# High and low weights of a two-block model, stored element by element in turn

## The chip, the cores and the metric

The kernel runs on one core of one Trainium2 chip. The metric is the device time in microseconds (us) of one execution; for the kernel before it is 2099.25 us, the median of three runs (2098.92 to 2099.32).

## The reference

The program computes two model blocks on 512 tokens of width 1024, all in f32. The first block normalises the input, projects it, and mixes the tokens three ways side by side (a gated recurrence in chunks, attention over neighbours on a grid, attention over 256 memory tokens). It merges the three with gates and adds a feed-forward part of width 2816. The second block has a short convolution mixer, another feed-forward part, an attention with forgetting gates and a last feed-forward part. Cut to the form that matters here:

```python
proj = rms_norm(x, mix_norm_g) @ w_in            # 1024 x 7184
...
x = x + merged @ w_out
x = x + (gelu(dwconv3(a)) * u) @ w_down          # a, u = split(h @ w_up)
...
x = x + (b * causal_dwconv(c * h)) @ a_w_out     # second block
k, v, f = split(rmsnorm(x) @ w_kvf)
x = x + (attention(q, k, v, f) * sigmoid(g)) @ b_w_out
```

Nearly all arithmetic is in the products of activations with weight matrices, and these must keep almost f32 accuracy.

## The kernel before

**Products.** TensorE multiplies in f32 rounded (F32R, printed fp32r), one column per cycle, with fewer bits than f32. To keep accuracy, each operand is split into a high part (rounded to F32R) and a low part (the rest). A product is then three matmuls that add up in the same PSUM bank: high weight x high input, high weight x low input, low weight x high input (L1652, L1653, L1654 in `unit`). Smaller products, such as attention scores and transposes, are plain f32, which TensorE streams at half that pace.

**Units.** A weight matrix is cut into units of 128 partitions x 1024 elements (512 KB): eight blocks of 128 x 128. For each block, TensorE loads a 128 x 128 weight block as its stationary operand (LDWEIGHTS, engine PEld) and streams 512 tokens of input through it (MATMUL, engine PE). A unit is thus 24 matmuls and 24 weight loads. There are 366 units, in the order in which the model needs them; the unit of the three-way merge is half as long in places, and the down projection's units have seven or eight blocks.

**The path of a unit.** Four slots (`NSLOT`) hold units in flight. SP starts the transfer of a unit into `RAW` when GpSimd has finished with the unit four before it (`lo_ready`). ScalarE copies it to the high part `WH`, which rounds it (`hi`, L655), as soon as the transfer has landed and TensorE has finished with the unit four before it (`unit_done`). GpSimd computes the low part `WL` = `RAW` - `WH` in four pieces of 256 elements (`lo`, L519). Then TensorE runs `unit`. All of it is ordered by semaphores and each engine's program is written out in order; no planner moves work.

**The tiles of the change.** `WH` and `WL` are two tiles of 128 partitions x 4 slots x 1024 elements, so that the 128 weights of a block lie in 512 contiguous bytes of a partition. Everything that touches them: `hi` (L655) and its variants for the output projection of the second block (L932, L940) write `WH`; `lo` (L519) and its variants (L529 for the forget gates, L540 for the gates of the recurrence, L628) read `WH` and write `WL` or a spare part of `WH`; the matmuls of L1652 to L1654, L1770 and L1771, L1828 to L1853, L1889 to L1891, L1949 and L1950, and L2049 to L2051 load them as the stationary operand.

One stage uses them the other way round. `value_blocks` (L1965 to L1967) makes the attention's values with tokens as rows. There, input blocks `XH` and `XL` are stationary, and 512 columns of `WH` or `WL` are the moving operand; these eight units are numbered from `U["fv"]`.

Of the kernel before, what the change touches and what calls it, by code (L numbers as in the profile page):

```python
# [12 lines left out]
F32 = mybir.dt.float32  # L13
F32R = mybir.dt.float32r
ALU = mybir.AluOpType
ACT = mybir.ActivationFunctionType
AX = mybir.AxisListType

P = 128
D = 1024  # L20
KB = D // P
# [6 lines left out]
NSLOT = 4  # L28
LO_PARTS = 4
UW = KB * P  # L30
# [119 lines left out]
U, O = {}, {}  # L150
# [38 lines left out]
def two_blocks(nc, A, out):  # L189
# [4 lines left out]
    def fixed(name, shape, dt=F32):  # L194
        t = nc.alloc_sbuf_tensor_at(name, shape, dt, offset=top[0])
        n = 4
        for d in shape[1:]:
            n *= d
        top[0] += (n + 31) // 32 * 32
        return t  # L200
# [13 lines left out]
    XH = fixed("XH", [P, KB, S], F32R)  # L214
    XL = fixed("XL", [P, KB, S], F32R)
    RAW = fixed("RAW", [P, NSLOT, UW])
    WH = fixed("WH", [P, NSLOT, UW], F32R)
    WL = fixed("WL", [P, NSLOT, UW], F32R)
    R = fixed("R", [P, S])
    RM = fixed("RM", [P, M])  # L220
    SS = fixed("SS", [P, S])
# [81 lines left out]
    bank = [nc.alloc_psum_tensor(f"bank{b}", [P, S], F32) for b in range(8)]  # L303
# [11 lines left out]
    hi_ready, lo_ready, unit_done = sem("hi_ready"), sem("lo_ready"), sem("unit_done")  # L315
# [67 lines left out]
    def width(u):  # L383

        j = u - U["merge"]
        return UW // 2 if 0 <= j < len(MRG) and MRG[j][0] == "br" else UW

    def blk(t, n):

        return t[:, bass.ds(n, 1), :].rearrange("p o s -> p (o s)")  # L390
# [121 lines left out]
    def _(pool):  # L512
        def lo(u0, j, i, per):
            s = (u0 + j) % NSLOT
            pool.wait_ge(hi_ready, i * per + (u0 + j + 1))
            parts = LO_PARTS * width(u0 + j) // UW
            for c in range(parts):
                w = slice(c * UW // LO_PARTS, (c + 1) * UW // LO_PARTS)
                last = nc.gpsimd.tensor_tensor(WL[:, s, w], RAW[:, s, w], WH[:, s, w].bitcast(F32), ALU.subtract)  # L519
                if u0 == 0 and j < 2 and c < parts - 1:  # L520
                    last.then_inc(first_lo[j], 1)
            last.then_inc(lo_ready, 1)

        def lo_forget():

            s = U["f"] % NSLOT
            pool.wait_ge(hi_ready, U["f"] + 1)
            raw, w = (t[:, s, :].rearrange("p (k c) -> p k c", c=P) for t in (RAW, WH))
            nc.gpsimd.tensor_tensor(w[:, :, 32:48], raw[:, :, 0:16], w[:, :, 0:16].bitcast(F32), ALU.subtract)\  # L529
                .then_inc(lo_ready, 1)  # L530

        def lo_gate(u):

            s = u % NSLOT
            pool.wait_ge(hi_ready, u + 1)
            raw, w = (t[:, s, :].rearrange("p (n c) -> p n c", c=32) for t in (RAW, WH))
            pool.wait_ge(r_ready, 1)
# [27 lines left out]
        for u in range(NATT):  # L565
# [4 lines left out]
            if u in BIAS_UNITS:  # L570

                p, v = BIAS_UNITS[u]
# [50 lines left out]
        def lo_parted(n):  # L623
# [3 lines left out]
            for w in [slice(c * 2 * P, min((c + 1) * 2 * P, KEND)) for c in range(LO_PARTS)]:  # L627
                nc.gpsimd.tensor_tensor(WL[:, s, w], RAW[:, s, w], WH[:, s, w].bitcast(F32), ALU.subtract)  # L628
            nc.gpsimd.tensor_tensor(WEL[:, n, :], RAW[:, s, KEND:UW], WEH[:, n, :].bitcast(F32), ALU.subtract)\
# [14 lines left out]
    def _(act):  # L644
        A_ = nc.scalar.activation

        def hi(u0, j, i, per):

            if not isinstance(i, int) or u0 + j + i * per < NUNITS:
                s = (u0 + j) % NSLOT  # L650
                act.wait_ge(raw_full[s], i * (16 * per // NSLOT) + 16 * ((u0 + j) // NSLOT + 1))
                if u0 + j >= NSLOT:
                    act.wait_ge(unit_done, i * per + (u0 + j - NSLOT + 1))
                w = slice(0, width(u0 + j))
                A_(WH[:, s, w], RAW[:, s, w], ACT.Copy).then_inc(hi_ready, 1)  # L655

        AHEAD = 3
        LN_EXP = "natural_log_exp_and_others"
# [51 lines left out]
        for t, (un, st) in enumerate(SLOTS):  # L710
            u = UIDX[un] if un else None
# [20 lines left out]
            if m < 4 * ML_H:  # L732

                h, s = m // 4, m % 4
# [8 lines left out]
                for d in range(2):  # L743
                    w = slice(P * s, S) if d == 0 else slice(0, P * (s + 1))
                    A_(SXM[m % 2][:, d, w], UE[:, h, d, w], ACT.Relu, bias=UT[:, s, 32 * d + h:32 * d + h + 1])
                act.drain()
                for d in range(2):
                    w = slice(P * s, S) if d == 0 else slice(0, P * (s + 1))
                    e = SXM[m % 2][:, d, w]
                    last = A_(e, e, ACT.Exp, scale=-1.0)  # L750
# [24 lines left out]
            if 1 in finishing(st):  # L775
                h = st[1] - 1
# [9 lines left out]
                for q in range(TB):  # L786
                    last = A_(HQ[:, q, :], HQ[:, q, :], ACT.Copy, scale=HS[:, q:q + 1])
                last.then_inc(h_rs, 1)
            if un and un[0] in HALF:
                k = sum(1 for x in UNITS[:u] if x[0] in HALF)  # L790
# [10 lines left out]
            if t and EXTRA[t - 1][:1] and EXTRA[t - 1][0][:2] == ("tr", "nav"):  # L801

                p = EXTRA[t - 1][0][2]
# [121 lines left out]
        def hi_parted(n):  # L925
# [4 lines left out]
            if n == 0:  # L930
                act.wait_ge(fc_out, 16)
            A_(WH[:, s, 0:KEND], RAW[:, s, 0:KEND], ACT.Copy)  # L932
            A_(WEH[:, n, :], RAW[:, s, KEND:UW], ACT.Copy).then_inc(hi_ready, 1)
# [700 lines left out]
    def _(pe):  # L1634
        mm = nc.tensor.matmul

        def unit(u0, j, i, per, kc, xh, xl, k0, dst, start=True, stop=True, width=S, ready=None, halfway=None):
# [4 lines left out]
            for k in range(kc):  # L1642
# [10 lines left out]
                mm(dst[:, 0:width], WH[:, s, w], b, start=False, stop=False)  # L1653
                last = mm(dst[:, 0:width], WL[:, s, w], a, start=False, stop=stop and k == kc - 1)  # L1654
            last.then_inc(unit_done, 1)
# [118 lines left out]
        for t, (un, st) in enumerate(SLOTS):  # L1774
            before = SLOTS[t - 1][1] if t else None
            if st and st[0] in ("xa", "na"):
                kind, p, s = st
# [3 lines left out]
                for j in range(2):  # L1781
                    if g >= 1:
                        pe.wait_ge(s_read, 2 * g + j - 1)
                    if kind == "xa":
                        h = 2 * p + j
                        mm(SB[j][:, 0:M], XQ[:, h, P * s:P * (s + 1)], MK[:, h, :], start=True, stop=True)\
                            .then_inc(s_full, 1)
                    else:
                        r = slice(64 * j, 64 * j + 64)
                        mm(SB[j][:, 0:M], QN[r, p % 2, P * s:P * (s + 1)], KN[r, p % 2, KEY0[s]:KEY0[s] + M],  # L1790
                           start=True, stop=True)\
                            .then_inc(s_full, 1)
            if st and st[0] == "ml":
                _, h, s = st
# [17 lines left out]
            if un:  # L1812
# [5 lines left out]
                if t == 0:  # L1818
                    for n, (tt, part, ks) in enumerate(START_ORDER):
# [3 lines left out]
                        for k in ks:  # L1823
                            w = slice(k * P, (k + 1) * P)
                            ends = n == START_LAST[tt] and k == KB - 1
                            if part == "h":
                                pe.wait_ge(xh_ready, k + 1)
                                last = mm(bb[:], WH[:, tt, w], XH[:, k, :], start=k == 0, stop=False)  # L1828
                            elif part == "l":
                                pe.wait_ge(split_ready, k + 1)  # L1830
                                last = mm(bb[:], WH[:, tt, w], XL[:, k, :], start=False, stop=ends)
                            else:
                                if tt < 2 and k < KB - 2:
                                    pe.wait_ge(first_lo[tt], k // 2 + 1)
                                else:
                                    pe.wait_ge(lo_ready, tt + 1)
                                last = mm(bb[:], WL[:, tt, w], XH[:, k, :], start=False, stop=ends)
                        if n == START_LAST[tt]:
# [5 lines left out]
                elif t < 5:  # L1844
                    b = mixer_bank(o)
                    pe.wait_ge(hi_ready, t + 1)
                    for k in range(KB):
                        w = slice(k * P, (k + 1) * P)
# [3 lines left out]
                    for k in range(KB):  # L1852
                        last = mm(b[:], WL[:, t % NSLOT, k * P:(k + 1) * P], XH[:, k, :], start=False, stop=k == KB - 1)  # L1853
# [99 lines left out]
        def value_blocks(h, u, blocks):  # L1953

            n = 4 * h + u
            slot = (U["fv"] + n) % NSLOT
            pe.wait_ge(lo_ready, U["fv"] + n + 1)
            for t in blocks:
                if h and u == 0:
                    pe.wait_ge(f_v, t + 1)  # L1960
                for kk in range(2):
                    k = 2 * u + kk
                    a, b = XH[:, k, t * P:(t + 1) * P], XL[:, k, t * P:(t + 1) * P]
                    w = slice(kk * S, (kk + 1) * S)
                    mm(bank[2 + t][:], a, WH[:, slot, w], start=k == 0, stop=False)  # L1965
                    mm(bank[2 + t][:], b, WH[:, slot, w], start=False, stop=False)  # L1966
                    last = mm(bank[2 + t][:], a, WL[:, slot, w], start=False, stop=k == KB - 1)  # L1967
                if t == TB - 1:
                    last.then_inc(unit_done, 1)
                elif u == 3:  # L1970
                    last.then_inc(v_full, 1)
# [96 lines left out]
        for t in range(TB):  # L2068
            last = mm(bank[6][:, 2 * t:2 * t + 2], SS[:, t * P:(t + 1) * P], ONES[:, 0:2], start=True, stop=True)
# [149 lines left out]
```

## Time and profile before

| what | value |
|---|---|
| median of three runs | 2099.25 us |
| span of the profiled execution, first to last instruction | 2098.1 us |
| TensorE matmul busy (PE) | 2090.3 us, 100% |
| TensorE weight load busy (PEld) | 1709.4 us, 81% |
| VectorE, ScalarE, GpSimd busy | 46%, 42%, 56% |
| matmuls, weight loads | 9860, 9860 |

The profile was taken in one execution. Its own time is the span, 2098.1 us, and what lies around it; the median of the runs is 1.15 us above the span. Records of matmuls overlap, because the next one begins to stream before the results of the one before are out, so the price of a matmul in a dense stretch is the distance from start to start, and not the length of its record. A weight load's record lies beside the matmul before it.

### The profile page before, as it was taken

How to read it: one execution, taken by the hardware profiler on the slowest of the kernel's cores; microseconds unless marked ns; L12 is line 12 of the kernel's file. 1: busy time of each engine (PE TensorE's matmuls, PEld its weight loads, DVE VectorE, ACT ScalarE, POOL GpSimd, SP SyncE). 2: the span in 40 equal slices, each digit the busy share in tenths (PEclk: the TensorE clock that was granted, in tenths of full speed). 3: DMA queues.
4: the chain of work that ended last, by engine and by line, in shares of the span. 5: the costliest groups of instructions: out<-in, count | busy, mean ns of one | idle time of the engine just before them, and what ended most of it. 6: DMA issues, size and time to landing. Idle time of an engine off the chain costs nothing.

```text
span 2098.1 us, 29633 instructions
## 1 busy us (share of the span) xinstructions
PE 2090.3 (100%) x9860; PEld 1709.4 (81%) x9860; DVE 972.7 (46%) x1682; ACT 884.3 (42%) x1355; POOL 1164.5 (56%) x1554
## 2 busy tenths in 40 slices
PE   9999999999999999999999999999999999999999
PEld 7788888888888888888888888888777778888887
DVE  6567564334455551234445544213377755545300
ACT  5544556223434343332244344224466655434321
POOL 8553346556555556555455656565544536556653
PEclk9999999999999999999999999999999999999999
DMA  6333222323332333323233333333322213333332
GB/s 234 119 99 114 63 64 70 106 78 123 92 100 93 96 94 102 95 91 100 91 101 100 96 94 89 108 94 101 111 81 81 81 61 101 100 100 90 103 92 76
DMA packets 62667, 203.70 MB, mean 97 GB/s; under 512 B 7056, under 2 KB 8720, under 8 KB 62576
## 3 DMA queue, kind: packets, MB, share of 16 engines
q1 hardware_dynamic: 60624, 201.54, 30.9%
q10 hardware_dynamic: 1952, 0.99, 0.2%
q8 instruction: 52, 0.85, 0.2%
q14 instruction: 39, 0.32, 0.0%
HBM read 199.42 MB, written 2.26 MB: 96 GB/s over the span
## 4 chain that ended last, share of the span: by engine, by line
PE 98%; DVE 1%; DMA 0%; DVEq 0%; ACT 0%; issue 0%; ACTq 0%; SPq 0%
PE bank L1652 28%; PE bank L1654 28%; PE bank L1653 28%; PE bank L1992 1%; PE bank L2018 1%; PE bank L1761 1%; PE bank L2004 1%; PE bank L1706 1%; PE bank L1965 1%; PE bank L1967 1%; PE bank L1966 1%; PE bank L1891 1%; PE bank L1889 1%; PE bank L1890 1%; PE bank L2049 1%; PE bank L1802 1%
## 5 line engine op out<-in xcount | busy, mean ns | idle before, releaser
L519 POOL TENSOR_TENSOR WL<-RAW,WH 128x256 fp32r<-128x256 f32 x1424 | 1105.8, 809 | 865.7 <-ACT WH L655 858.8
L1652 PE MATMUL bank<-XH,WH 128*128 128x512 f32 x1688 | 661.2, 392 | 0.3 <-DVE FG L1571 0.3
L1654 PE MATMUL bank<-XH,WL 128*128 128x512 f32 x1688 | 657.2, 389 | 0.0
L1653 PE MATMUL bank<-XL,WH 128*128 128x512 f32 x1688 | 656.9, 389 | 0.0
L655 ACT ACTIVATE WH<-RAW 128x1024 fp32r<-128x1024 f32 (+1 forms) x366 | 372.9, 1023 | 236.1 <-PE bank L1654 208.4
L1652 PEld LDWEIGHTS bank<-XH,WH 128*128 128x128 f32 x1688 | 316.9, 188 | 68.4 <-issue 2.8
L1654 PEld LDWEIGHTS bank<-XH,WL 128*128 128x128 f32 x1688 | 316.9, 188 | 66.7
L1653 PEld LDWEIGHTS bank<-XL,WH 128*128 128x128 f32 x1688 | 317.0, 188 | 64.5
L1652 PE MATMUL bank<-FH,WH 128*128 128x512 f32 x528 | 205.4, 389 | 0.0
L1653 PE MATMUL bank<-FL,WH 128*128 128x512 f32 x528 | 205.4, 389 | 0.0
L1654 PE MATMUL bank<-FH,WL 128*128 128x512 f32 x528 | 205.4, 389 | 0.0
L1399 DVE TENSOR_TENSOR X<-X,bank 128x512 f32 (+1 forms) x48 | 32.9, 685 | 292.4 <-PE bank L1654 283.9
L882 ACT ACTIVATE TD<-TC 128x512 f32<-128x512 f32 x66 | 41.7, 632 | 278.0 <-DVE TC L1143 188.0
L1143 DVE SCALAR_TENSOR_TENSOR TC<-TA,PAR,TC 128x511 f32<-128x511 f32 (+1 forms) x134 | 108.9, 813 | 22.4 <-issue 21.8
L1653 PEld LDWEIGHTS bank<-FL,WH 128*128 128x128 f32 x528 | 99.1, 188 | 20.7
L1654 PEld LDWEIGHTS bank<-FH,WL 128*128 128x128 f32 x528 | 99.1, 188 | 20.7
L1652 PEld LDWEIGHTS bank<-FH,WH 128*128 128x128 f32 x528 | 99.1, 188 | 20.4
L1429 DVE TENSOR_TENSOR TA<-bank,R 128x512 f32<-128x512 f32 x66 | 45.6, 691 | 124.1 <-PE bank L1654 116.1
L1434 DVE TENSOR_TENSOR TE<-bank,R 128x512 f32<-128x512 f32 x66 | 45.6, 691 | 110.0 <-PE bank L1654 110.0
L885 ACT ACTIVATE FH<-TA 128x512 f32 x66 | 41.8, 633 | 126.3 <-DVE TA L1438 126.3
L1440 DVE TENSOR_TENSOR FL<-TA,FH 128x512 f32 x66 | 60.1, 911 | 61.7 <-ACT FH L885 61.7
L849 ACT ACTIVATE XH<-X,PAR (+1 forms) x40 | 29.0, 724 | 134.9 <-DVE X L1399 134.9
(336 smaller groups left out, 2618.5 us busy)
## 6 DMA issues: line engine op xcount, KB each, us to landing
RAW<-in_w_up SPq DMA_DIRECT2D x132, 512.0 KB, 3.5
RAW<-in_w_att SPq DMA_DIRECT2D x50, 512.0 KB, 3.6
RAW<-in_w_down SPq DMA_DIRECT2D x48, 448.0 KB, 3.2
RAW<-in_w_down SPq DMA_DIRECT2D x24, 512.0 KB, 3.5
RAW<-in_w_ain SPq DMA_DIRECT2D x24, 512.0 KB, 3.4
RAW<-in_w_fa SPq DMA_DIRECT2D x24, 512.0 KB, 3.6
RAW<-in_w_mrg SPq DMA_DIRECT2D x15, 512.0 KB, 3.9
RAW<-in_w_mrg SPq DMA_DIRECT2D x24, 256.0 KB, 2.7
```

What stands on the lines that cost most here:

```text
L519: last = nc.gpsimd.tensor_tensor(WL[:, s, w], RAW[:, s, w], WH[:, s, w].bitcast(F32), ALU.subtract)
L655: A_(WH[:, s, w], RAW[:, s, w], ACT.Copy).then_inc(hi_ready, 1)
L882: A_(TD[:], TC[:], fn).then_inc(glu_ready, 1)
L885: A_(blk(FH, i * 2 + n), TA[:], ACT.Copy).then_inc(ffh_ready, 1)
L1143: last = v.scalar_tensor_tensor(out=TC[:, -d:S], in0=c[:, 0:S + d], scalar=w[k], in1=TC[:, -d:S], op0=ALU.mult, op1=ALU.add)
L1399: v.tensor_tensor(blk(X, nn), blk(X, nn), b[:], ALU.add).then_inc(lin_free, 1)
L1429: v.tensor_tensor(TA[:], LB[0 if (O[name] % 2) == 0 else 1][:], R[:], ALU.mult)\
L1434: v.tensor_tensor(TE[:], LB[1 if (O[name] % 2) == 0 else 0][:], R[:], ALU.mult)\
L1440: v.tensor_tensor(blk(FL, nn), TA[:], blk(FH, nn).bitcast(F32), ALU.subtract).then_inc(ffl_ready, 1)
L1652: mm(dst[:, 0:width], WH[:, s, w], a, start=start and k == 0, stop=False)
L1653: mm(dst[:, 0:width], WH[:, s, w], b, start=False, stop=False)
L1654: last = mm(dst[:, 0:width], WL[:, s, w], a, start=False, stop=stop and k == kc - 1)
```

## The change

High and low weights share one tile, `WHL`, of 2 x 1024 elements a slot. Element 2n is the high part of weight n, element 2n + 1 its low part; `WH` and `WL` become views with a step of two elements, 8 bytes. Every access through these names now steps 8 bytes: ScalarE's writes, GpSimd's reads and writes, and TensorE's weight loads. For the eight units of the value blocks the same memory is used in two contiguous halves, `WPH` and `WPL`; a helper, `weights`, picks the views by the unit's number. The tiles take as much memory as before. No instruction, wait or transfer is added, removed or moved.

```diff
-    WH = fixed("WH", [P, NSLOT, UW], F32R)
-    WL = fixed("WL", [P, NSLOT, UW], F32R)
+    WHL = fixed("WHL", [P, NSLOT, 2 * UW], F32R)
+    WPAIR = WHL[:].rearrange("p s (n h) -> p s n h", h=2)
+    WH, WL = WPAIR[:, :, :, 0], WPAIR[:, :, :, 1]
+    WPH, WPL = WHL[:, :, 0:UW], WHL[:, :, UW:2 * UW]
...
+    def weights(u):
+
+        return (WPH, WPL) if U["fv"] <= u < U["fa"] else (WH, WL)
...
-                last = nc.gpsimd.tensor_tensor(WL[:, s, w], RAW[:, s, w], WH[:, s, w].bitcast(F32), ALU.subtract)
+                h, l = weights(u0)
+                last = nc.gpsimd.tensor_tensor(l[:, s, w], RAW[:, s, w], h[:, s, w].bitcast(F32), ALU.subtract)
...
-                A_(WH[:, s, w], RAW[:, s, w], ACT.Copy).then_inc(hi_ready, 1)
+                A_(weights(u0 + j + (i * per if isinstance(i, int) else 0))[0][:, s, w], RAW[:, s, w], ACT.Copy).then_inc(hi_ready, 1)
...
-                    mm(bank[2 + t][:], a, WH[:, slot, w], start=k == 0, stop=False)
-                    mm(bank[2 + t][:], b, WH[:, slot, w], start=False, stop=False)
-                    last = mm(bank[2 + t][:], a, WL[:, slot, w], start=False, stop=k == KB - 1)
+                    mm(bank[2 + t][:], a, WPH[:, slot, w], start=k == 0, stop=False)
+                    mm(bank[2 + t][:], b, WPH[:, slot, w], start=False, stop=False)
+                    last = mm(bank[2 + t][:], a, WPL[:, slot, w], start=False, stop=k == KB - 1)
```

## Rows read from the trace of the kernel before

**Rows 1.** The page: span, engine totals (busy us, share, instructions), chain by engine.

```profile
span 2098.1 us, 29633 instructions
PE 2090.3 (100%) x9860; PEld 1709.4 (81%) x9860; DVE 972.7 (46%) x1682; ACT 884.3 (42%) x1355; POOL 1164.5 (56%) x1554
...
PE 98%; DVE 1%; DMA 0%; DVEq 0%; ACT 0%; issue 0%; ACTq 0%; SPq 0%
```

**Rows 2.** The page's costliest groups: xcount, busy us, mean ns, idle before, releaser.

```profile
L519 POOL TENSOR_TENSOR WL<-RAW,WH 128x256 fp32r<-128x256 f32 x1424 | 1105.8, 809 | 865.7 <-ACT WH L655 858.8
L1652 PE MATMUL bank<-XH,WH 128*128 128x512 f32 x1688 | 661.2, 392 | 0.3 <-DVE FG L1571 0.3
...
L655 ACT ACTIVATE WH<-RAW 128x1024 fp32r<-128x1024 f32 (+1 forms) x366 | 372.9, 1023 | 236.1 <-PE bank L1654 208.4
L1652 PEld LDWEIGHTS bank<-XH,WH 128*128 128x128 f32 x1688 | 316.9, 188 | 68.4 <-issue 2.8
```

**Rows 3.** Timeline of PE, from 1000 us: start us, length us.

```profile
1000.06 0.39 PE L1652 MATMUL bank<-XH,WH 128*128 128x512 f32 x1
...
1003.46 0.39 PE L1652 MATMUL bank<-XH,WH 128*128 128x512 f32 x1
```

**Rows 4.** Span and mean granted TensorE clock.

```profile
core 0: 2098.1 us, clock 1.000
```

**Rows 5.** Timeline of PEld in the same stretch.

```profile
1000.06 0.19 PEld L1653 LDWEIGHTS bank<-XL,WH 128*128 128x128 f32 x1
```

**Rows 6.** Timeline of PE, plain f32 matmuls, two in each row.

```profile
907.85 1.02 PE L1666 MATMUL bank<-TC,ONER 128*128 128x512 f32 x2
908.71 1.02 PE L1668 MATMUL bank<-SS,ONER 128*128 128x512 f32 x2
```

**Rows 7.** Timeline of PE, 256 columns: a matmul and the eighth after it.

```profile
84.08 0.28 PE L1652 MATMUL bank<-MH,WH 128*128 128x256 f32 x1
...
85.04 0.28 PE L1654 MATMUL bank<-MH,WL 128*128 128x256 f32 x1
```

**Rows 8.** A pause: L1891 from 505 us (min/median/max ns), timelines of PE and PEld.

```profile
L1891 PE MATMUL bank<-GH,WL x5: 388/389/389, 504.7 to 507.4; 128*128 128x512 f32 x5
...
507.38 0.39 PE L1891 MATMUL bank<-GH,WL 128*128 128x512 f32 x1
507.99 0.50 PE L1652 MATMUL bank<-GH,WH 128*128 128x512 f32 x1 [0.22 <-DVE X L1399]
...
507.99 0.19 PEld L1652 LDWEIGHTS bank<-GH,WH 128*128 128x128 f32 x1 [0.64 <-DVE X L1399]
508.10 0.19 PEld L1653 LDWEIGHTS bank<-GL,WH 128*128 128x128 f32 x1
```

**Rows 9.** The first matmul of L1828 alone, and timelines of PE and PEld there.

```profile
L1828 PE MATMUL bank<-XH,WH x1: 473/473/473, 7.3 to 7.3; 128*128 128x512 f32 x1
...
7.34 1.02 PE L1828 MATMUL bank<-XH,WH 128*128 128x512 f32 x2 [0.89 <-ACT XH L685]
...
7.31 0.19 PEld L1828 LDWEIGHTS bank<-XH,WH 128*128 128x128 f32 x1 [1.05 <-issue]
7.86 0.19 PEld L1828 LDWEIGHTS bank<-XH,WH 128*128 128x128 f32 x1 [0.36 <-ACT XH L685]
```

**Rows 10.** View by tile, matmuls that read WH: duration ns min/median/max, first and last start.

```profile
L1653 PE MATMUL bank<-XL,WH x1688: 387/389/402, 38.7 to 1974.5; 128*128 128x512 f32 x188
...
L1653 PE MATMUL bank<-AHL,WH x176: 387/389/402, 1044.3 to 1667.4; 128*128 128x512 f32 x176
...
L1965 PE MATMUL bank<-WH,XH x64: 389/389/486, 1436.3 to 1484.3; 128*128 128x512 f32 x64
```

**Rows 11.** Weight loads of 48 columns.

```profile
L1949 PEld LDWEIGHTS bank<-XH,WH 128*48 128x48 f32 x8 | 1.0, 122 | 0.8
```

**Rows 12.** GpSimd subtractions of 512 elements: contiguous, and in runs of 16.

```profile
L589 POOL TENSOR_TENSOR YL<-Y,YH 128x512 fp32r<-128x512 f32 x8 | 10.1, 1285 | 15.2 <-ACT YH L770 15.2
L540 POOL TENSOR_TENSOR WH<-RAW,WH 128x512 fp32r<-128x512 f32 x1 | 1.3, 1283 | 0.1
```

## The prediction

> **What bounds the kernel now.** I read the engine totals and the chain of waits first. TensorE is busy for 2090.3 of 2098.1 us, and 98% of the chain that ended last is TensorE itself: at almost no point does it wait for weights, for a transfer or for another engine [rows 1]. So only two things can move the time: the distance from one matmul to the next, or an engine beside TensorE becoming slower than TensorE.
>
> Next the costliest groups. The three matmuls of a weight block (high weight with high input, high with low, low with high) make up nearly everything; each has a weight load of its own, 188 ns long, beside a matmul whose record is 389 ns long [rows 2]. Records overlap, so the real price of a matmul is the distance of starts: from 1000.06 to 1003.46 us lie 15 matmuls, 3.40 us / 15 = 226.7 ns each [rows 3]. The granted clock is 1.000 over the span, the 2.4 GHz level [rows 4], so 512 columns at one per cycle would be 512 / 2.4 = 213.3 ns. Each matmul thus has 13.3 ns, 32 cycles, that are not columns. These 13.3 ns are the only thing on the path that a different weight layout can touch.
>
> Whose are they? The load of the next block starts with the matmul before it: L1653's load at 1000.06 us, with L1652's matmul [rows 3, 5]. So it runs inside that stream. Three places tell something.
> - Matmuls of plain f32, which take two cycles a column, have almost none of it: from 907.85 to 908.71 us two of them, 430 ns each, against 1024 / 2.4 = 426.7 [rows 6]. They too have a load beside them. So a load beside a stream is not dear by itself.
> - With 256 columns in fp32r the distance is (85.04 - 84.08) / 8 = 120 ns against 106.7 for the columns [rows 7]. Again 13.3 ns: the surplus goes with the matmul, not with its length. And a load every 120 ns is sustained, so a load occupies its path for 120 ns at most.
> - The last matmul before a pause, at 507.38 us, has no load beside it, since the next block is taken up at 507.99. If the load beside it were what lengthens a stream, its record should be some 13 ns shorter. It has the shortest of its window, 388 ns against 389 [rows 8]. Likewise the matmul at 7.34 us: its own load starts at 7.31, the next load at 7.86, after the 473 ns of its record; from its load's start to its end that is 0.50 us [rows 9]. The matmul at 507.99 starts with its load, has the next load inside it from 508.10 on, and ends after the same 0.50 us [rows 8].
>
> So the surplus looks like a fixed price at the start of an fp32r matmul, and not like something that the load of the next block takes from it. That speaks for no change. It is not proof: records of the same matmul spread from 387 to 402 ns [rows 10], so something in the meeting of loads and streams does vary, and ends are modelled.
>
> **The change part by part.**
> *Weight loads.* Each L1652 to L1654 has 1688 + 528 + 176 + 96 + 64 + 48 = 2600 loads, one for each matmul in the view by tile [rows 10] (two of its six groups are shown), three lines 7800; L2049 to L2051, L1889 to L1891 and the first units add 524. So 8324 of 9860 loads now step 8 bytes. The 192 matmuls of the value blocks keep contiguous weights as moving operand (64 at each of three lines) [rows 10]; the norm sums, transposes and attention products load other tiles. No load or matmul is added. Each nanosecond on the distance is worth 8.3 us, 0.4%.
> The trace has no load with a step, so I bound it. What a load costs per column: 48 columns take 122 ns, 128 take 188 [rows 2, 11], so (188 - 122) / 80 = 0.83 ns a column. Lower end: 0, the step costs nothing. Upper end: every column twice, 106 ns more, a record of 294 ns. The path of the load would then be taken for 120 + 106 = 226 ns out of 226.7: just hidden. If its fixed part doubled too, 240 ns, 13.3 ns a matmul would come out on the path, 111 us. I take 0, since the room for even a doubling is there.
>
> *ScalarE.* It writes the high weights at a step of 8 bytes. A copy takes 1023 ns, the mean over full and half units [rows 2]. A unit of 24 matmuls lasts 24 x 226.7 = 5.44 us on TensorE. Doubled, 2.1 us: still hidden, since ScalarE is at 42% [rows 1] and works up to three units ahead in four slots. I take 0.
>
> *GpSimd.* It reads the high weights and writes the low ones at 8 bytes, four pieces a unit, 809 ns each [rows 2], 3.24 us of 5.44. It becomes the bound from 5.44 / 4 = 1360 ns a piece, in the 21-matmul units of the down projection from 21 x 226.7 / 4 = 1190 ns. The nearest row with a broken pattern is the gate unit, 512 elements in runs of 16 with gaps: 1283 ns, against 1285 for 512 contiguous [rows 12]. So a gap costs nothing there; the lower end is 0, the upper end a doubling, 1618 ns. I take 0, by that row.
> The Trainium skill, GPSIMD Engine Reference, section 7 (Performance pitfalls for Q7 kernels), charges about half more for reads whose step is over 8 bytes and nothing up to 8, which this change just meets. If the chip charged it here all the same, a piece would be 809 x 1.5 = 1214 ns, hidden everywhere but in the down units, where 4 x 1214 - 4760 = 96 ns on 72 units would show as 7 us at most; by the rule itself the term is 0. No run here shows such a read.
>
> *Slots, transfers, waits.* Four slots as before; transfers land in the raw tile, which is untouched. No wait is added or moved, so nothing new stands behind one.
>
> Sum: 0 on loads + 0 on ScalarE + 0 on GpSimd. The profiled execution's span is 2098.1 us; the median of the runs is 2099.25, 1.15 above it. Forecast 2099.2 us, with a range of its own of 2096 to 2103.
>
> **The rivals.**
> *Loads and streams get in each other's way less (faster).* The 32 cycles are a quarter of 128 columns, and 128 weights of 4 bytes are 32 pieces of 16 bytes: the price could be one cycle for each place where the load and the moving read meet, and a load that walks through memory at twice the pace could meet it in another rhythm. For it: plain f32, which reads its moving operand at half the pace, has hardly any surplus [rows 6], and the records spread [rows 10]. Against it: the matmuls without a load beside them are no shorter [rows 8, 9]. Price: all of it 13.3 x 8324 = 111 us, 1988; down to the surplus of plain f32 (3 ns) 86 us, 2013; I put this case at half, 6.7 ns, 55 us: 2044.
>
> *The same meeting costs more (slower).* If the price goes by the stretch of memory that a load covers, 1024 bytes in place of 512 make 64 cycles of surplus: a distance of 240 ns, 13.3 x 8324 = 111 us, 2210; if half of the new pieces are dodged, 2155. It decides from the first nanosecond, on every unit's matmuls alike. For and against it the same rows speak as before, and the path of the load that could just take a doubling ends at the same 240 ns.
> The Trainium skill, SBUF — State Buffer, section Specifications (TRN2), has lines of 16 bytes, wants two hits in each for full bandwidth, and says that each crossing to a new line pays a penalty. A step of 8 bytes keeps two hits, by which the forecast holds; it also crosses twice as often, by which this rival does. No run here shows lines.
>
> *GpSimd becomes the bound (slower).* At 1618 ns a piece a unit takes 6.47 us, 1.03 more than its matmuls, on some 350 units 360 us: 2460. It decides from 1360 ns, a factor of 1.68. Against it the gate unit's row [rows 12].
>
> **How the numbers follow.** No change: 0.42. Less in each other's way: 0.30. More: 0.23. GpSimd: 0.05. Within 0.2% (4 us, about what a measurement of this kernel can tell from none) is the forecast's own case, 0.42; faster 0.30; slower 0.23 + 0.05 = 0.28. For a range that holds 8 in 10, I take the halves of both middle rivals and some way past them, 2030 to 2185; outside are a full gain (about 0.06), a full doubling (about 0.09) and GpSimd.
>
> **What would show it.** The distance of matmul starts in the same stretch: 226.7 ns if the forecast is right, 213 to 222 for the first rival, 232 to 240 for the second. The load's record: 188 ns if the step is free, up to 294 if columns are read twice. GpSimd's piece: near 809 ns, and TensorE waiting for GpSimd in the chain only if it passes 1360. The value blocks, whose loads stay contiguous, must keep 226.7 in every case; if they move as well, the reason is not the load's step.

## The result, and the profile after

| kernel | median us | span of the profiled execution, us |
|---|---|---|
| before | 2099.28 (2098.92 to 2099.50, 4 runs) | 2098.1 |
| after | 2150.65 (2150.14 to 2151.05, 4 runs) | 2149.1 |

The ratio is 1.0244, with an interval of 1.0230 to 1.0259: slower by 51 us, where no change was forecast. One execution of e8 below (3389.49 us, at a mean granted clock of 0.577) fell in a slow state and stands in no comparison. The line numbers of the kernel after are those of before plus 7 (L1652 is L1659, L519 is L526), and high and low weights carry one name, `WHL`.

The page of after: engine totals and chain, then the costliest groups (count, busy us, mean ns of one, idle before). They answer to [rows 1, 2].

```profile
PE 2142.2 (100%) x9860; PEld 1754.9 (82%) x9860; DVE 975.8 (45%) x1682; ACT 912.7 (42%) x1355; POOL 1172.2 (55%) x1554
...
PE 99%; DVE 1%; DMA 0%; ACT 0%; DVEq 0%; issue 0%; SPq 0%; ACTq 0%
...
L526 POOL TENSOR_TENSOR WHL<-RAW,WHL 128x256 fp32r<-128x256 f32 x1424 | 1113.6, 814 | 907.6 <-ACT WHL L662 901.9
L1659 PE MATMUL bank<-XH,WHL 128*128 128x512 f32 x1688 | 669.3, 397 | 0.3 <-DVE FG L1578 0.3
...
L662 ACT ACTIVATE WHL<-RAW 128x1024 fp32r<-128x1024 f32 (+1 forms) x366 | 401.2, 1100 | 241.5 <-PE bank L1661 213.3
L1659 PEld LDWEIGHTS bank<-XH,WHL 128*128 128x128 f32 x1688 | 326.1, 193 | 70.2 <-issue 2.8
```

TensorE still is the whole chain, and no other engine has come near it: GpSimd's piece went from 809 to 814 ns, ScalarE's copy from 1023 to 1100, the weight load's record from 188 to 193. So the distance of matmuls must have grown. The timeline of PE in after, where [rows 3] stand for before:

```profile
1000.17 0.39 PE L1659 MATMUL bank<-XH,WHL 128*128 128x512 f32 x1
...
1003.67 0.39 PE L1659 MATMUL bank<-XH,WHL 128*128 128x512 f32 x1
```

15 matmuls take 3.50 us: 233.3 ns each, against 226.7. The granted clock is 1.000 as before (2.4 GHz), so 544 cycles have become 560. Which matmuls moved is read from the view by tile (record ns min/median/max, first and last start), whose rows answer to [rows 10]:

```profile
L1660 PE MATMUL bank<-XL,WHL x1688: 392/394/399, 39.4 to 2022.1; 128*128 128x512 f32 x188
...
L1660 PE MATMUL bank<-ML,WHL x64: 278/283/288, 84.9 to 143.5; 128*128 128x256 f32 x64
...
L1972 PE MATMUL bank<-WHL,XH x64: 389/389/486, 1472.9 to 1520.9; 128*128 128x512 f32 x64
```

Records of 512 columns went from 389 to 394 ns. The value blocks (L1972), whose stationary operand is still contiguous, kept 389 ns. Their distance in the timeline of PE in after is (1493.65 - 1490.25) / 15 = 226.7 ns, as before:

```profile
1490.25 0.39 PE L1972 MATMUL bank<-WHL,XH 128*128 128x512 f32 x1
...
1493.65 0.39 PE L1972 MATMUL bank<-WHL,XH 128*128 128x512 f32 x1
```

The 256-column matmuls have stepped loads too, yet kept the distance of 120 ns of [rows 7]: in the timeline of PE in after, (85.49 - 84.89) / 5 = 120 ns.

```profile
84.89 0.28 PE L1660 MATMUL bank<-ML,WHL 128*128 128x256 f32 x1
...
85.49 0.28 PE L1659 MATMUL bank<-MH,WHL 128*128 128x256 f32 x1
```

The sum closes. Some 8045 dense distances of 512-column matmuls that load stepped weights, times 6.67 ns, are 53.7 us. Against that the matmuls just after a pause lose less than before: counted over the trace, these distances in sum lay 2.5 us above 226.7 ns each in before and 0.2 us below 233.3 ns each in after. 53.7 - 2.7 = 51.0 us; the spans differ by 51.0.

### The profile page after: what moved, and what is told of

Same layout as the page of the kernel before. It is cut to its first block, busy times and chain, and to the rows that moved or that the text cites. A ratio compares the mean times of both kernels' runs of the same rounds, so it can differ in the third digit from the quotient of the medians.

```text
span 2149.1 us, 29633 instructions
## 1 busy us (share of the span) xinstructions
PE 2142.2 (100%) x9860; PEld 1754.9 (82%) x9860; DVE 975.8 (45%) x1682; ACT 912.7 (42%) x1355; POOL 1172.2 (55%) x1554
## 4 chain that ended last, share of the span: by engine, by line
PE 99%; DVE 1%; DMA 0%; ACT 0%; DVEq 0%; issue 0%; SPq 0%; ACTq 0%
PE bank L1659 28%; PE bank L1661 28%; PE bank L1660 28%; PE bank L1999 1%; PE bank L2025 1%; PE bank L1768 1%; PE bank L2011 1%; PE bank L1713 1%; PE bank L2056 1%; PE bank L1972 1%; PE bank L1974 1%; PE bank L1898 1%; PE bank L1973 1%; PE bank L1896 1%; PE bank L1897 1%; PE bank L2058 1%
## 5 line engine op out<-in xcount | busy, mean ns | idle before, releaser
L526 POOL TENSOR_TENSOR WHL<-RAW,WHL 128x256 fp32r<-128x256 f32 x1424 | 1113.6, 814 | 907.6 <-ACT WHL L662 901.9
L1659 PE MATMUL bank<-XH,WHL 128*128 128x512 f32 x1688 | 669.3, 397 | 0.3 <-DVE FG L1578 0.3
L1661 PE MATMUL bank<-XH,WHL 128*128 128x512 f32 x1688 | 665.2, 394 | 0.0
L1660 PE MATMUL bank<-XL,WHL 128*128 128x512 f32 x1688 | 665.2, 394 | 0.0
L662 ACT ACTIVATE WHL<-RAW 128x1024 fp32r<-128x1024 f32 (+1 forms) x366 | 401.2, 1100 | 241.5 <-PE bank L1661 213.3
L1659 PEld LDWEIGHTS bank<-XH,WHL 128*128 128x128 f32 x1688 | 326.1, 193 | 70.2 <-issue 2.8
L1661 PEld LDWEIGHTS bank<-XH,WHL 128*128 128x128 f32 x1688 | 326.0, 193 | 67.8
L1660 PEld LDWEIGHTS bank<-XL,WHL 128*128 128x128 f32 x1688 | 326.1, 193 | 66.1
L1661 PE MATMUL bank<-FH,WHL 128*128 128x512 f32 x528 | 208.0, 394 | 0.0
L1659 PE MATMUL bank<-FH,WHL 128*128 128x512 f32 x528 | 208.0, 394 | 0.0
L1660 PE MATMUL bank<-FL,WHL 128*128 128x512 f32 x528 | 208.0, 394 | 0.0
L1659 PEld LDWEIGHTS bank<-FH,WHL 128*128 128x128 f32 x528 | 101.9, 193 | 21.4
L1660 PEld LDWEIGHTS bank<-FL,WHL 128*128 128x128 f32 x528 | 101.9, 193 | 21.3
L1661 PEld LDWEIGHTS bank<-FH,WHL 128*128 128x128 f32 x528 | 101.9, 193 | 21.2
```

The source lines that it names most:

```text
L526: last = nc.gpsimd.tensor_tensor(l[:, s, w], RAW[:, s, w], h[:, s, w].bitcast(F32), ALU.subtract)
L662: A_(weights(u0 + j + (i * per if isinstance(i, int) else 0))[0][:, s, w], RAW[:, s, w], ACT.Copy).then_inc(hi_ready, 1)
L1659: mm(dst[:, 0:width], WH[:, s, w], a, start=start and k == 0, stop=False)
```

## The experiments

All times are set against the kernel before on the same chip. In e1 and e2, theory A lays the price on the loads and theory B on the copies. From e3 on, the expectations weigh two kinds of theory about the loads: a toll (the theories A), which each load pays for its own step, and a pattern (theory B), by which the load's addresses and the moving operand's reads fall into a rhythm with more or fewer waits.

### e1: loads contiguous again, copies stepped

```diff
-                mm(dst[:, 0:width], WH[:, s, w], a, start=start and k == 0, stop=False)
-                mm(dst[:, 0:width], WH[:, s, w], b, start=False, stop=False)
-                last = mm(dst[:, 0:width], WL[:, s, w], a, start=False, stop=stop and k == kc - 1)
+                mm(dst[:, 0:width], WPH[:, s, w], a, start=start and k == 0, stop=False)
+                mm(dst[:, 0:width], WPH[:, s, w], b, start=False, stop=False)
+                last = mm(dst[:, 0:width], WPL[:, s, w], a, start=False, stop=stop and k == kc - 1)
```

(and so at L1896 to L1898 and L2056 to L2058)

> The changed kernel, but 8172 of its 8324 stepped weight loads read 512 contiguous bytes of the slot; both copies still write at 8 bytes (so the weights that are multiplied are not the matrix's). Theory A, the load's step lengthens the stream by 6.7 ns: the distance goes back to 226.7 ns and the time to 2099 + 152 x 6.7 ns = 2100 us. Theory B, the stepped copies of ScalarE and GpSimd disturb TensorE's reads: distance 233.3 ns, time 2150 us as in the changed kernel.

Measured: 2099.89 us, ratio 1.0002 (0.9993 to 1.0012). The page of e1, GpSimd and ScalarE, and a row of its view by tile:

```profile
L526 POOL TENSOR_TENSOR WHL<-RAW,WHL 128x256 fp32r<-128x256 f32 x1424 | 1120.8, 819 | 851.5 <-ACT WHL L662 846.2
L662 ACT ACTIVATE WHL<-RAW 128x1024 fp32r<-128x1024 f32 (+1 forms) x366 | 399.7, 1096 | 229.7 <-PE bank L1661 202.6
...
L1659 PE MATMUL bank<-FH,WHL x528: 388/389/390, 781.0 to 2094.2; 128*128 128x512 f32 x176
```

Both engines pay for their steps as in after (819 and 1096 ns), while the matmuls' records and the time are those of before. So the copies cost the kernel nothing that shows, and the price is with the loads.

### e2: copies contiguous, loads stepped

```diff
-        return (WPH, WPL) if U["fv"] <= u < U["fa"] else (WH, WL)
+        return (WH, WL) if u < 5 else (WPH, WPL)
```

(and both copies ask for the views of each unit's own number)

> The counterpart: the loads step 8 bytes as in the changed kernel, the copies of all units from the sixth on write contiguous halves (the weights that are multiplied are again not the matrix's). Theory A, the load's step: distance 233.3 ns, time about 2150 us. Theory B, the copies: 226.7 ns, about 2100 us.

Measured: 2149.95 us, ratio 1.0241 (1.0224 to 1.0259), with ScalarE's copy back at 1023 ns. The view by tile:

```profile
L1659 PE MATMUL bank<-FH,WHL x528: 394/394/394, 797.2 to 2144.0; 128*128 128x512 f32 x176
```

The mirror image of e1: with the copies contiguous but for the first units, the stepped loads alone make the whole price (50.5 us over the kernel before on the same chip).

### e3: a sweep of TensorE alone

35 stretches of 48 dense matmuls each, all else left out. `w(offset, (step, count))` is the load, `m(...)` the moving operand, in elements of 4 bytes; both tiles lie on the same grid.

```python
for i in R: last = mm(bank[0][:], w(128 * (i % 8), (1, P)), m(512 * (i % 8), (1, S)), start=i == 0, stop=i == N - 1)
for i in R: last = mm(bank[1][:], w(256 * (i % 8), (2, P)), m(512 * (i % 8), (1, S)), start=i == 0, stop=i == N - 1)
```

> Only streams on TensorE, 35 stretches of 48 matmuls one behind the other, each with its own load; no other engine works beside them and the model is not computed. Theory A1, a toll by the stretch of memory that the load covers, 16 cycles for each 512 bytes on top of 16 fixed: step 1, 2, 3, 4, 5, 6, 8 give 226.7, 233.3, 240, 246.7, 253, 260, 273 ns, step 0 gives 220, 64 columns at step 1 give 223; the direction of the moving operand changes nothing. Theory A2, a toll by 16-byte lines touched, at most one per column: as A1 up to step 4, then constant at 246.7. [...] In the stretch where only every fourth load steps 16 bytes, the distance that is longer is that of the matmul during which this load runs if the load takes from the stream beside it, and that of its own matmul if the stream waits for it.

The timeline of PE in e3. A row joins 32 matmuls: start, and time from the first start to the last end; less one record, over the steps between the starts, it is the distance (L53: (7.63 - 0.39) / 31 = 233.5 ns). The table's values come from the unrounded starts.

```profile
34.66 7.63 PE L53 MATMUL bank<-X,W 128*128 128x512 f32 x32
...
45.89 7.70 PE L54 MATMUL bank<-X,W 128*128 128x512 f32 x32
...
80.19 7.58 PE L57 MATMUL bank<-X,W 128*128 128x512 f32 x32
...
169.64 7.63 PE L65 MATMUL bank<-X,W 128*128 128x512 f32 x32
...
240.12 14.69 PE L71 MATMUL bank<-X,W 128*128 128x512 f32 x32
...
346.71 7.07 PE L79 MATMUL bank<-X,W 128*128 128x512 f32 x32
...
357.32 7.63 PE L80 MATMUL bank<-X,W 128*128 128x512 f32 x32
...
374.27 7.63 PE L82 MATMUL bank<-X,W 128*128 128x256 f32 x32
...
448.95 7.42 PE L86 MATMUL bank<-X,W 128*128 128x512 f32 x32
```

Mean distance of the 17th to 48th start in each stretch:

| load | moving operand | line | distance, ns |
|---|---|---|---|
| contiguous | ascending | L86 | 226.7 |
| step 8 bytes | ascending | L53 | 233.3 |
| step 12, 16, 32 bytes | ascending | L54 to L56 | 235.6, 235.1, 245.4 |
| one address | ascending | L57 | 231.7 |
| contiguous, 64 or 32 columns | ascending | L62, L64 | 230.2, 231.7 |
| contiguous, 8 bytes later | ascending | L60 | 230.7 |
| contiguous, 8 bytes, 16 bytes, one address | descending | L65 to L68 | 233.3 each |
| contiguous | one address | L79 | 215.8 |
| step 16 bytes | one address | L80 | 233.3 |
| step 16 bytes | ascending, 256 columns | L82 | 233.3 |
| contiguous | step 8 bytes | L71 | 453.2 |

The sweep repeats the kernel's two numbers with TensorE alone (226.7 and 233.3), so nothing else in the kernel is needed. The tolls fall: a load from one address, or of a quarter of the columns, should be the cheapest, and is dearer than the contiguous one; with a descending stream the load's step is indifferent; a contiguous load that merely begins 8 bytes later is dearer. With one load in four at a step of 16 bytes (L84) no fourth distance stands out, neither of the two that the expectation names: all lie between 231 and 235 ns, 233.4 in the mean. And where the moving operand is one address, 215.8 ns remain, 518 cycles for 512 columns: all but 6 cycles of the surplus go with the walk of the moving operand. The step of 16 bytes has a limit of its own besides: such loads follow each other every 233.3 ns, whether 256 columns or a single moving address stand against them (L82, L80).

### e4: a third of the loads contiguous

```diff
-                last = mm(dst[:, 0:width], WL[:, s, w], a, start=False, stop=stop and k == kc - 1)
+                last = mm(dst[:, 0:width], WPL[:, s, w], a, start=False, stop=stop and k == kc - 1)
```

(and so at L1898 and L2058)

> The changed kernel, but the loads of the low weights, one in three, read 512 contiguous bytes (not the matrix's weights). Theory A, each stepped load lengthens the stream beside it by 6.7 ns, independently of its neighbours: the distance after the second matmul of a block, during which the contiguous load runs, is 226.7 ns, the other two 233.3; about 2150.6 - 2724 x 6.7 ns = 2132.5 us. Theory A', the price falls on the load's own matmul: the same time, but the distance after the third is the short one. Theory B, the distances are a rhythm that a load's pattern pulls the stream into: no distance need be 226.7 or 233.3, and the time need not lie at a third of the way.

Measured: 2148.52 us, ratio 1.0232 (1.0215 to 1.0249). A price per stepped load would have given back a third of it, 2132.5. The timeline of PE in e4:

```profile
849.95 0.39 PE L1659 MATMUL bank<-FH,WHL 128*128 128x512 f32 x1
...
852.75 0.39 PE L1659 MATMUL bank<-FH,WHL 128*128 128x512 f32 x1
```

2.80 us for four blocks, 12 matmuls: 233.3 ns each. The stream as a whole keeps its distance when one load in three is contiguous. So the price is not a sum over the stepped loads, as a toll would have it.

### e5: more of the sweep

39 stretches: columns, moving orders, offsets, types. The lines for 384 columns with a stepped load and for weights that begin 64 bytes late:

```python
for i in R: last = mm(bank[1][:, 0:384], w(256 * (i % 8), (2, P)), m(512 * (i % 8), (1, 384)), start=i == 0, stop=i == N - 1)
...
for i in R: last = mm(bank[4][:], w(16 + 128 * (i % 8), (1, P)), m(512 * (i % 8), (1, 512)), start=i == 0, stop=i == N - 1)
```

> Only streams on TensorE again, 39 stretches of 48 matmuls. (1) Moving operand from a single address, loads at step 2: if the surplus is waiting in the moving operand's reads, 216 ns as for step 1; if the load alone makes it, 222 to 223. (2) 448, 384, 320, 256 columns: if the surplus is a fixed price per matmul, as the prediction has it, 200, 173.3, 146.7, 120 ns at step 1; if it goes with the columns (17 cycles for 16), 198.3, 170, 141.7, 113.3 ns unless the load is the limit. At step 2: 13.3 ns less per 32 columns either way, from 233.3. (3) bf16 and plain f32, whose moving operand needs half the bytes in a given time: no more than 3 ns between contiguous loads and loads at 8 bytes, if the surplus is a matter of how fast the moving operand is read. (4) Other offsets and other orders of the moving operand's columns: a theory of a fixed price has 226.7 and 233.3 everywhere; a theory of meetings has other values, and some may lie below 226.7.

The timeline of PE in e5: 512 columns with a contiguous and a stepped load (L55, L56), one moving address with a stepped load (L58), 384 columns with either (L60, L64), bf16 with either (L89, L90), plain f32 with a stepped one (L92).

```profile
27.00 7.42 PE L55 MATMUL bank<-X,W 128*128 128x512 f32 x32
37.99 7.63 PE L56 MATMUL bank<-X,W 128*128 128x512 f32 x32
...
59.28 7.07 PE L58 MATMUL bank<-X,W 128*128 128x512 f32 x32
...
78.76 5.88 PE L60 MATMUL bank<-X,W 128*128 128x384 f32 x33
...
109.64 5.88 PE L64 MATMUL bank<-X,W 128*128 128x384 f32 x33
...
381.94 7.07 PE L89 MATMUL bank<-XB,WB 128*128 128x512 bf16 x32
392.30 7.07 PE L90 MATMUL bank<-XB,WB 128*128 128x512 bf16 x32
...
446.85 13.90 PE L92 MATMUL bank<-X,W 128*128 128x512 f32 x32
```

The step of 8 bytes is free in bf16 (215.8 ns both ways), in plain f32 (429.2 both ways), with one moving address (215.8 both ways) and at 384, 320 and 256 columns (173.3, 146.7, 120.0 both ways). At 448 columns the stepped load is even the cheaper one, 203.3 against 206.7 ns. So of these streams only those in fp32r whose moving operand walks have something to lose, and how much depends on the length of the stream as well. With contiguous loads, operands moved against each other by 256, 512 or 1024 bytes kept 226.7; weights moved by 64 bytes went to 233.4 without any step (L75). Eleven other orders of the moving operand's columns (L78 to L88) had 226.7 to 277.7 ns; none was shorter than the plain ascending one. Where contiguous and stepped loads alternate, the mean is 230.2 ns (L67), which a sum of tolls would give too (230.0); with one stepped load in four it is 231.7 (L68), where the sum gives 228.3.

### e6: the layout of before, 32 bytes off the grid

```diff
+    top[0] = (top[0] + line - 1) // line * line - 32
+    WH = fixed("WH", [P, NSLOT, UW], F32R)
+    WL = fixed("WL", [P, NSLOT, UW], F32R)
+    RC = fixed("RC", [P, 2 * TB])
     top[0] = (top[0] + line - 1) // line * line
     X = fixed("X", [P, KB, S])
```

(their old places are removed)

> The kernel before with contiguous weights, both weight tiles moved as a whole to lie 32 bytes lower against the 512-byte grid on which the input tiles lie; nothing else changes and the model is computed in full. Theory A, the step of the load costs the 6.7 ns: no step, so 226.7 ns and 2099 us. Theory B, the distance depends on how the load's addresses meet the moving operand's: the sweep's nearest stretch (moving operand 32 bytes higher, step 1) had 233.3 ns, so about 2099 + 8324 x 6.6 ns = 2154 us, as slow as the changed kernel without any step.

Measured: 2150.40 us, ratio 1.0242 (1.0225 to 1.0259). The timeline of PE in e6:

```profile
1000.02 0.39 PE L1653 MATMUL bank<-XH,WH 128*128 128x512 f32 x1
...
1003.52 0.40 PE L1653 MATMUL bank<-XH,WH 128*128 128x512 f32 x1
```

3.50 us over 15 matmuls: 233.3 ns, without one of the change's stepped accesses. The price of the change can thus be had without the change: what counts is where the load's addresses lie against the moving operand's.

### e7: where the weights begin

36 stretches over the load's first address (48 elements are 192 bytes) and over lengths of 464, 480 and 496 columns:

```python
for i in R: last = mm(bank[4][:], w(48 + 128 * (i % 8), (1, P)), m(512 * (i % 8), (1, 512)), start=i == 0, stop=i == N - 1)
...
for i in R: last = mm(bank[5][:], w(16 + 256 * (i % 8), (2, P)), m(512 * (i % 8), (1, 512)), start=i == 0, stop=i == N - 1)
```

> Only streams on TensorE, 36 stretches of 48 matmuls, loads at step 1 and step 2 with 25 starting offsets, and 496, 480 and 464 columns. Theory A, a price of the step: every step 1 has 226.7 ns, every step 2 has 233.3. Theory B, a meeting by address: step 1 has 226.7 only for offsets that are a multiple of 256 bytes and 228 to 234 at others; if it can be won as well as lost, some offset lies below 226.7 (220 would be 16 cycles of surplus in place of 32), and that offset would be worth 6.7 ns x 8324 = 55 us in the model's kernel.

Measured, contiguous load beginning so many bytes past the 256-byte grid: 0: 226.7; 4: 232.5; 8: 230.8; 16 to 112: 231.9 to 234.4; 128 and 160: 233.5; 192: 228.9; 224: 233.3; 240: 226.7; 256 and 768: 226.7 ns. With the step of 8 bytes: 0, 16, 96, 256, 512: 233.3; 8: 231.7; 32: 231.9; 64: 230.0; 128: 231.4; 192: 233.5. With 496, 480 and 464 columns: 220.0, 216.7 and 208.8 ns contiguous, 225.3, 220.0 and 211.6 with the step. At 512 columns none of the starts and steps tried gave less than 226.7, so the sweep offered no better layout to run. The timeline of PE in e7: 192 bytes past the grid (L64), 240 past it (L66), stepped 64 past it (L73), stepped 256 past it (L77).

```profile
157.04 7.48 PE L64 MATMUL bank<-X,W 128*128 128x512 f32 x32
...
179.18 7.42 PE L66 MATMUL bank<-X,W 128*128 128x512 f32 x32
...
256.55 7.52 PE L73 MATMUL bank<-X,W 128*128 128x512 f32 x32
...
301.15 7.63 PE L77 MATMUL bank<-X,W 128*128 128x512 f32 x32
```

### e8 and e9: two starts from the sweep, in the whole kernel

e8 is e6 with 64 in place of 32 (192 bytes past a 256-byte mark; one more small tile fills the gap); e9 is the kernel after with its tile moved likewise:

```diff
+    top[0] = (top[0] + line - 1) // line * line - 192
+    WHL = fixed("WHL", [P, NSLOT, 2 * UW], F32R)
```

(its views follow it, and its old place is removed)

> The kernel before with contiguous weights, its high and low weights put 64 bytes below the 512-byte grid on which the inputs lie (the whole model is computed). Theory B (the address pattern of the load against the moving operand's reads sets how often the stream waits, and the pattern counts as in the third sweep): 64 bytes below the grid is 192 bytes past the last 256-byte mark, where the sweep had 228.9 ns; the shift by 32 bytes turned 6.6 ns on the distance into 51 us, so 2.2 ns give 17 us, 2116 us. Rival (on the grid 226.7 ns, off it 233.3, nothing between in a whole kernel whose three matmuls read different inputs): 2150 us. Rival (only distances below 64 bytes count): 2099 us.

> The changed kernel with the shared tile put 192 bytes below the 512-byte grid, that is 64 bytes past a 256-byte mark; weight loads still step 8 bytes (the whole model is computed). Theory B: the third sweep had 230.0 ns for a step of 8 bytes at this start, 3.3 ns above 226.7 and half of what the step costs on the grid, so about 2099 + 25 = 2125 us: faster than the changed kernel by an address alone. The value blocks, whose moving operand is shifted too, go from 226.7 to about 228.9 ns (first sweep, moving operand 64 bytes past). Rival (the step costs by itself, wherever the tile lies): 2150.7 us and value blocks at 226.7.

Measured: e8 ran 2116.35, 2119.40 and 2124.06 us, ratio 1.0087 (1.0065 to 1.0108); e9 2127.88 (2127.53 to 2129.49), ratio 1.0134 (1.0116 to 1.0152). The medians, 2119.40 and 2127.88, lie 3 us above what the sweep gave and far from 2150; and e9 makes the changed kernel 23 us faster by an address alone. That the tiles stand in another order in e6 is not its price: e8 has the same order. The value blocks fit too: in e6 and e8, where their moving operand is the shifted tile, their distance went from 226.7 to 233.3 ns. What the sweep had not shown stands in the timeline of PE in e8, the same line and tiles in the first feed-forward part and in the second:

```profile
699.61 0.40 PE L1653 MATMUL bank<-XH,WH 128*128 128x512 f32 x1
...
703.11 0.40 PE L1653 MATMUL bank<-XH,WH 128*128 128x512 f32 x1
...
1200.20 0.39 PE L1653 MATMUL bank<-XH,WH 128*128 128x512 f32 x1
...
1203.64 0.39 PE L1653 MATMUL bank<-XH,WH 128*128 128x512 f32 x1
```

3.50 / 15 = 233.3 ns in the one, 3.44 / 15 = 229.3 in the other. From 549 to 920 us the stream keeps 233.3 from one pause to the next; elsewhere mostly 228.9. e9 does the same with 233.3 (352 to 514 and 922 to 1059 us) and 230.0, and the changed kernel has short stretches of 235.5 (343 to 353 us). One layout can settle in two rhythms, and in these profiles it changed only across a pause. The profiled execution of e8, 2124.06 us, is 8 us above the sweep's figure, and the long stretch makes 7 of them (1592 distances, 4.4 ns each); that of e9, 2129.49 us, is 4 above, and its two stretches make 4 (1283 distances, 3.3 ns each). The differences between e8's runs may be of the same kind; the others have no profile. The value blocks of e9, whose moving operand is shifted against its stationary one, went to about 229 ns as expected; the timeline of PE in e9:

```profile
1470.11 0.39 PE L1973 MATMUL bank<-WHL,XH 128*128 128x512 f32 x1
...
1473.54 0.39 PE L1973 MATMUL bank<-WHL,XH 128*128 128x512 f32 x1
```

(3.43 / 15 = 228.7.)

## Why the prediction was wrong

**The step that failed.** "So the surplus looks like a fixed price at the start of an fp32r matmul, and not like something that the load of the next block takes from it." From this the loads were priced at 0, "since the room for even a doubling is there": the load was bounded by how long it keeps its own path busy, and not by what its addresses do to the stream beside it. The term measured 51 us, 6.67 ns on each distance of 512 columns (e1, e2). Of the 32 cycles of surplus in before, 6 are there when the moving operand stands still (215.8 ns); the other 26 go with its walk, and 16 more come with the load's addresses (e3, e6).

**Why the evidence misled.**
- Plain f32 [rows 6] was read as: a load beside a stream is harmless. It is harmless there even with a step (429.2 ns, e5), as it is in bf16. By the distances, both read about 2 bytes of moving operand a cycle and fp32r nearly 4 (each plain f32 product leaves two records of 429 ns, 96 for 48 products in e5, so it takes four cycles a column in all); that this is why they are spared fits, but was not tested. The row said nothing on fp32r.
- The 256 columns [rows 7] were read as: the surplus is the same at every length. With contiguous loads the sweeps have 32 surplus cycles at 256, 320, 384, 496 and 512 columns, but 48 at 448 (496 cycles), 40 at 480 and 37 at 464. Two lengths that agreed hid that.
- The matmuls without a load beside them [rows 8, 9] kept their record of 388 ns, where the stream with one moving address has 379 (L79, L58). So these rows may even be right that the 26 cycles need no load; no experiment ran a stream without loads. They could not tell what another load pattern would add.

**What spoke against it and was passed over.** The prediction saw the records spread from 387 to 402 ns [rows 10] and went on. Where they spread was to be seen in the kernel before, right behind the pause of [rows 8], in the timeline of PE:

```profile
508.33 0.40 PE L1653 MATMUL bank<-GL,WH 128*128 128x512 f32 x1
...
510.88 0.39 PE L1652 MATMUL bank<-GH,WH 128*128 128x512 f32 x1
...
512.92 0.39 PE L1652 MATMUL bank<-GH,WH 128*128 128x512 f32 x1
```

From 508.33 to 510.88 lie 11 distances of 231.8 ns, from there to 512.92 nine of 226.7: same tiles, same clock, same loads. 226.7 is what the stream settles to, not what a matmul costs. The matmuls of the very loads of [rows 11], 48 contiguous columns, say it more plainly, in the timeline of PE in before:

```profile
1440.38 0.40 PE L1949 MATMUL bank<-XH,WH 128*48 128x512 f32 x1
...
1441.32 0.40 PE L1949 MATMUL bank<-XH,WH 128*48 128x512 f32 x1
```

Four distances take 0.94 us, 235 ns each: these loads are 66 ns shorter than those of 128 columns, and the stream beside them is 8 ns a matmul slower. A fixed price would have left it at 226.7. With the step, in after, the same 16 matmuls have 230.3 ns.

**The load's room.** The room was there, and not needed: stepped loads at 256 columns follow each other every 120 ns as the contiguous ones do (e5), and the record grew by 5 ns, not 106. The near doubling that was priced comes at a step of 16 bytes (records of 310 ns, 330 at 32 bytes in e3; one load every 233.3 ns in place of 120), and even so 512 columns hide most of it (235.1 ns).

**The sums.** The 8324 loads that a nanosecond was multiplied by include 192 of 256-column matmuls, which lost nothing, and those at pauses; some 8045 remain. The 7 us set as a ceiling for GpSimd in the down projection count all 72 units, of which 48 have seven blocks, so it would be 5 us. Neither moves the forecast.

**The rivals.** "The same meeting costs more (slower)" had the sign and, at half price, the size: 2155 against 2150.65, and through it the range of 2030 to 2185 holds the result. That was luck: its mechanism, a price by the stretch of memory that a load covers, is not what was found. e6 covers the old 512 bytes and pays the same, and a load from a single address pays too (231.7). The first rival's "another rhythm" was the nearer picture, with the other sign. The Trainium skill, SBUF — State Buffer, section Specifications (TRN2), wants two hits in each 16-byte line. The load's own pace obeys it: 120 ns at 256 columns with the step of 8 bytes, 233.3 with 16. The stream does not: the same 8-byte step as moving operand doubles the distance (453.2 ns, L71), and it is e6, with none but contiguous loads of these weights, that loses as much as the change. The measurement decides: the rule prices neither.

**What held.** ScalarE's and GpSimd's terms are 0 on the path (e1), with 1100 ns against 1023 and 814 against 809. The Trainium skill, GPSIMD Engine Reference, section 7 (Performance pitfalls for Q7 kernels), charges for a read's step only above 8 bytes; the 814 ns agree. The value blocks kept 226.7. TensorE stayed the only bound.

**What stays open.** Shown is that the load's addresses against the moving operand's set the distance. By what mechanism they do it, why 544 and 560 cycles are so often the settled values, and whether a load is needed for the first 26 cycles, was not shown.

## What to carry to other kernels

In a dense fp32r stream the settled distance of starts depends on how weight loads lie against the moving operand: keep contiguous stationary and moving tiles on one grid of 256 bytes (226.7 ns here at each of its starts that was tried), and after a change of layout read the distance of starts beside the records. A surplus that is constant in two places is not yet a constant; look for places in the same trace where it isn't, just behind a pause and beside loads of another size. An engine's load that fits its own time slot can still slow the stream beside it, so bound both.

## What the runs showed of the hardware that was not expected

- A shift of contiguous weights by 32 bytes costs this kernel 2.4% (e6); 64 bytes 0.9% (e8).
- In the kernel before, loads of 48 contiguous columns go with 235 ns, those of 128 with 226.7.
- A stream can settle in either of two distances with the same addresses (229 or 233.3 ns in e8, 230.0 or 233.3 in e9) and keep it for up to 371 us (549 to 920 us in e8), until a pause.
- A moving operand in descending order costs 233.3 ns whatever the load's step; one that steps 8 bytes costs 453.2 ns; bf16 streams have 215.8 ns with and without a step of the load.
